# Eight projection slabs with a Gelu moved from the second attention into the stage of the recurrence

## The chip, the cores and the metric

The kernel runs on one core of one Trainium2 chip. A core has five engines, each working through its own queue in order: TensorE (PE) for matmuls, VectorE (DVE), ScalarE (ACT) for functions from tables, GpSimd (POOL) and SyncE (SP), which here issues the DMAs. They wait for one another by semaphores. The metric is the device time of one execution in microseconds, median of several.

## The reference

Two transformer-like blocks of width 1024 over 512 positions, in float32. The change lies in the first half of the second block:

```python
u, g_lru, q, k, v, z = jnp.split(rmsnorm(x) @ w_in, ...)   # 1024, 1024, 1024, 256, 256, 2048 wide
uc  = centred_depthwise_conv(u, conv_w, conv_b)
h   = rg_lru(uc, ..., reverse=False) + rg_lru(uc, ..., reverse=True)
y_a = h * gelu(g_lru)
y_b = banded_alibi_sink_attention(q, k, v, sink)           # 16 heads of 64, blocks of 128, neighbours on both sides
gates = sigmoid(z + b_gate)                                # two of 1024
x = x + (gates[0] * y_a + gates[1] * y_b) @ w_out
```

`rg_lru` is a gated linear recurrence over the positions: r and i are sigmoids of block-diagonal products of uc, a = exp(-8 r softplus(-lam)), b = sqrt(1 - a^2) i uc, h[t] = a[t] h[t-1] + b[t].

## The kernel before

All activations lie transposed, channels on the 128 partitions, 512 positions along a row, so a width of 1024 is eight tiles (DC = 8). Weights come as a stream of 232 slabs of 512 KB, each eight tiles of 128 x 128, in one fixed order (`ORDER`, L71). Each slab goes through four steps. SP loads it into `raw`, which has two places, once VectorE has done the split of the slab two before (L384 to 386). ScalarE rounds it into `w_hi` (`split`, L473), VectorE subtracts to get the rest `w_lo` (`split`, L782); these two have four places, and ScalarE's split also waits until the slab four before is multiplied (L479). TensorE multiplies high x high, high x low and low x high, 24 matmuls of 512 columns for eight tiles (`gemm`, L1371, matmuls L1386 to L1388), into one of the two banks of `gp`. It waits for `w_lo_ready` of the slab and for the output that last had the bank to be read (`FREED`, L278 to L290). Each engine calls its split of slab n + 2 (AHEAD = 2) where it comes to slab n in its own written order, so the order of calls in each engine's code is the order of the work. There is no planner.

The second attention works in 16 units (4 blocks of positions x 2 pairs of key heads x 2 halves). Unit u: scores of unit u + 2 on TensorE (L1509), logits and their maximum on VectorE (L1048 to L1059), exponentials on ScalarE (L563 to L567), transposes of the probabilities (L1537) copied by ScalarE (L588), the inverse of the sums spread over the partitions (L1520), the product with the values (L1548), the outputs copied by ScalarE (L572) and scaled by VectorE (L1070). Blocks 0 and 3 have two key blocks, 1 and 2 three. Between the units stands `between(u)`: one projection slab each. Even units take a tile of u: evacuation with the scale R (L1100) and convolution (L1260 to L1266). Odd units take a tile of g_lru: evacuation into G2 (L1254), ScalarE's Gelu on it (L684), and the split of the convolved tile into `h_hi` (L682) and `h_lo` (called at L1255, the operation is L821). TensorE's `between(u + 1)` stands ahead of the spread inverse and the value product of unit u (L1542). ScalarE runs `exponentials(u + 2)` and then `gate(u + 1)` (L593 to L596); VectorE runs `inverse_sums(u + 1)`, `outputs(u - 1)`, `logits(u + 2)` and then `between(u + 1)` (L1082 to L1092).

The stage of the recurrence goes over eight tiles t. The slabs come in the order `MIX` (L60): at even t one slab of recurrence gates for two tiles (`lru`), then `zb` of tile t, then `za` of tile t - 1. ScalarE (L700 to L732): wait until VectorE has freed the recurrence's buffers (`lru_free`), four sigmoids L710, two tanh L714, two exponentials L717, a square root L720 behind VectorE's clamp, then the splits and the gates' sigmoids (`mix_gate`, L693). VectorE (L1294 to L1323): clamp L1296, two products L1298, L1302, L1305, two scans L1307 and L1308, their sum L1309 (this increments `lru_free`), then the splits, the evacuations `gate_product` (L1279), the product with G2 (L1315), and `gated_attention` and `merged`. The recurrence's buffers `lru` exist once. Then `out2` multiplies the merged tiles by w_out, from `h_hi` and `h_lo`.

Of the kernel before, what the change touches and what calls it, by code (L numbers as in the profile page):

```python
# [20 lines left out]
ALU = mybir.AluOpType  # L21
# [32 lines left out]

_counts = [("u", 4), ("k", 1), ("v", 1), ("gate_a", 8), ("q", 4), ("gate_s", 8), ("branch_a", 4),
           ("glu", 2), ("branch_s", 4), ("out", 8), ("ff", 16 * FF1_PARTS),
           ("q2", 8), ("k2", 2), ("v2", 2), ("u2", 8), ("g2", 8), ("mix", 20),
           ("out2", 8), ("ff2", sum(2 * c + 8 for c in FF2_CHUNKS))]

MIX = []  # L60
for _t in range(DC):
    MIX += ([("lru", _t // 2)] if _t % 2 == 0 else []) + [("zb", _t)] + ([("za", _t - 1)] if _t else [])
MIX += [("za", DC - 1)]
SLAB, _n = {}, 0
for _name, _c in _counts:
    SLAB[_name] = _n
# [2 lines left out]
COUNT = dict(_counts)  # L69

ORDER = list(range(NSLAB))  # L71
for _k in range(8):
    ORDER[SLAB["u2"] + 2 * _k], ORDER[SLAB["u2"] + 2 * _k + 1] = SLAB["u2"] + _k, SLAB["g2"] + _k
assert NSLAB % RING == 0


_outs = [("u", 4), ("k", 1), ("v", 1), ("gate_a", 8), ("q", 4), ("gate_s", 8), ("branch_a", 8), ("glu", 4),
         ("branch_s", 8), ("out", 8), ("ff", 16 * FF1_PARTS), ("q2", 8), ("k2", 2), ("v2", 2), ("u2", 8),
         ("g2", 8), ("mix", 16), ("out2", 8), ("ff2", sum(2 * c + 8 for c in FF2_CHUNKS))]
OUT, _n = {}, 0  # L80
for _name, _c in _outs:
    OUT[_name] = _n
    _n += _c

MIX_SLAB = {key: SLAB["mix"] + i for i, key in enumerate(MIX)}
MIX_OUT = {key: OUT["mix"] + i for i, key in enumerate(k for k in MIX if k[0] != "lru")}

MIX_GATE = [g for t in range(1, DC + 1) for g in [("zb", t - 1)] + ([("za", t - 2)] if t > 1 else [])] + [("za", DC - 1)]


_cols = [("g_mix_pre", 8), ("g_mix_post", 8), ("g_mlp_pre", 8), ("g_mlp_post", 8), ("sinks", 8), ("d_skip", 4),
# [18 lines left out]
def build(nc, slabs, params, s5p, s5bt, s5b, s5c, bias1, nd2, x_in, out):  # L110

    ctx = ExitStack()
    with ctx:
# [152 lines left out]
        H_AT = {"z": 0, "y1": 4, "z2": 12, "ff": 16, "uc": 48, "m2": 56, "ff2": 64}  # L266
        V_AT = {"ff": 0, "uc": 32, "m2": 40, "ff2": 48}
        X_AT = {"post1": 0, "post2": 8, "ff2": 16}
        G_AT = {"gate_a": 0, "gate_s": 8, "g2": 16, "mix": 24, "ff2": 40}
        MIX_VAL = {key: G_AT["mix"] + i + 1 for i, key in enumerate(MIX_GATE)}  # L270
        PART1 = 2 * FF1_PART + DC - FF1_PART
        PART2 = 2 * FF2_CHUNKS[0] + DC
# [6 lines left out]
        for _name, _c in _outs:  # L279
            for _k in range(_c):  # L280
                _o = OUT[_name] + _k
                if _name in ("ff", "q2") and 2 <= _k < START_BANKS:
                    PLACE[_o] = mp, _k - 2
                elif _name in ("gate_s", "u2", "g2"):
# [17 lines left out]
        class Attention:  # L302
# [21 lines left out]
            def lanes(self, u):  # L324


                hp = self.units[u][2]
                return [(i, i % 2, 2 * hp + i // 2, 2 * (i % 2) + i // 2) for i in range(4)]

            def scores(self, i):  # L330
                return mp[:, i, :] if i < 3 else gp[:, 1, :]
# [138 lines left out]
        def _(act):  # L470
# [81 lines left out]
            def attention(A, slab0, gate):  # L552

                for pp in range(A.pairs):
                    act.wait_ge(vt_done, pp + 1 + (A.u0 > 0))
                    nc.scalar.activation(A.vt[:, pp, :, :].rearrange("p a b -> p (a b)"), mp[:, 3 + pp, :],
                                         ACT.Copy).then_inc(vt_ready, 1)

                def exponentials(u):
                    row = mini[u % 3]  # L560
                    lo, hi = A.span(u)
                    act.wait_ge(nb_ready, A.u0 + u + 1)
                    nc.scalar.activation(row[:, 3, :], row[:, 2, :], ACT.Exp)  # L563
                    for h in range(4):
                        L = A.logit[u % 2][:, h, lo:hi]
                        ins = nc.scalar.activation(L, L, ACT.Exp, bias=row[:, 1, h:h + 1], scale=0.125,  # L566
                                                   accum_out=row[:, 4, h:h + 1])  # L567
                    ins.then_inc(ex_done, 1)

                def take_outputs(u):  # L570
                    act.wait_ge(at_done, A.u0 + u + 1)
                    nc.scalar.activation(A.of_heads(A.q, u), by_heads(mp[:, 5, 0:2 * P]), ACT.Copy).then_inc(at_copied, 1)  # L572

                def outputs_hi(u):
                    act.wait_ge(at_read, A.u0 + u + 1)
                    nc.scalar.activation(A.of_heads(h_hi, u), A.of_heads(A.q, u), ACT.Copy).then_inc(h_hi_ready, 1)

                n = len(A.units)
                split(slab0 + AHEAD)
                exponentials(0)  # L580
                exponentials(1)
                gate(0)
                for u in range(n):
                    if u:
                        take_outputs(u - 1)
                    for g, j, _ in A.chunks[u]:
                        act.wait_ge(pt_done, g + 1)
                        nc.scalar.activation(A.pt[:, j, :], mp[:, 3 + g % 2, :], ACT.Copy).then_inc(pt_ready, 1)  # L588
                    if A.name and u:
                        outputs_hi(u - 1)  # L590
                    if u + 1 < n:
                        split(slab0 + u + 1 + AHEAD)
                    if u + 2 < n:  # L593
                        exponentials(u + 2)
                    if u + 1 < n:
                        gate(u + 1)  # L596
                take_outputs(n - 1)
                if A.name:
                    outputs_hi(n - 1)
# [77 lines left out]
            def inputs2(u):  # L677

                m = u // 2
                if u % 2:  # L680
                    act.wait_ge(h_val, V_AT["uc"] + m + 1)
                    nc.scalar.activation(h_hi[:, m, :], UC[:, m, :], ACT.Copy).then_inc(h_hi_ready, 1)  # L682
                    act.wait_ge(out_read, OUT["u2"] + u + 1)
                    nc.scalar.activation(G2[:, m, :], G2[:, m, :], ACT.Gelu_apprx_tanh).then_inc(gate_val, 1)  # L684
            attention(att2, SLAB["u2"], inputs2)


            act.wait_ge(decay_ready, 1)

            def mix_gate(kind, t):  # L690
                row, bias = {"za": (1, 0), "zb": (0, 8)}[kind]
                act.wait_ge(out_read, MIX_OUT[kind, t] + 1)
                nc.scalar.activation(tmp[row], tmp[row], ACT.Sigmoid, bias=col("b_gate", bias + t)).then_inc(gate_val, 1)  # L693
# [6 lines left out]
            for t in range(DC):  # L700
# [18 lines left out]
                act.wait_ge(lru_mid, t + 1)  # L719
                nc.scalar.activation(lru45, lru45, ACT.Sqrt).then_inc(lru_root, 1)  # L720

                split(MIX_SLAB["zb", t] + AHEAD)
                if t >= 1:
                    mix_gate("zb", t - 1)
# [53 lines left out]
        def _(dve):  # L778
# [471 lines left out]
            def inputs2(u):  # L1250

                m = u // 2
                if u % 2:
                    evacuate("u2", u, G2[:, m, :])  # L1254
                    h_low(H_AT["uc"] + m, m, UC[:, m, :])  # L1255
                    return
                x, y = tmp[m % 2], UC[:, m, :]
                evacuate("u2", u, x)
                dve.wait_ge(out_read, OUT["u2"] + u + 1)
# [8 lines left out]
            dve.wait_ge(decay_ready, 1)  # L1268
            dve.wait_ge(s_nd, 16)
            attention(att2, inputs2)  # L1270
            dve.wait_ge(gate_val, G_AT["g2"] + DC)
            dve.wait_ge(at_read, att2.u0 + len(att2.units))


            def gate_product(kind, t, row):

                split(MIX_SLAB[kind, t] + AHEAD)
                dve.wait_ge(half_done, 2 * (MIX_SLAB[kind, t] + 1))
                TT(row, gp[:, MIX_OUT[kind, t] % 2, :], R[:, :], ALU.mult).then_inc(out_read, 1)  # L1279

            def gated_attention(t):
                dve.wait_ge(gate_val, MIX_VAL["zb", t])
# [1 line left out]

            def merged(t):
                dve.wait_ge(gate_val, MIX_VAL["za", t])
                V.run(TT(HS[:, t, :], HS[:, t, :], tmp[1], ALU.mult))
                TT(Q2[:, t, :], Q2[:, t, :], HS[:, t, :], ALU.add).then_inc(h_val, 1)

# [2 lines left out]

            split(MIX_SLAB["lru", 0] + AHEAD)
            for t in range(DC):  # L1294
                dve.wait_ge(lru_tanh, t + 1)
                TS(lru45, lru45, 0.0, None, ALU.max).then_inc(lru_mid, 1)  # L1296
                for d in range(2):
# [10 lines left out]
                V.run(dve.tensor_tensor_scan(lru[5][:, ::-1], lru[2][:, ::-1], lru[3][:, ::-1], 0.0, ALU.mult, ALU.add))  # L1308
                TT(HS[:, t, :], HS[:, t, :], lru[5], ALU.add).then_inc(lru_free, 1)  # L1309

                if t >= 1:
                    gated_attention(t - 1)
                gate_product("zb", t, tmp[0])
                dve.wait_ge(lru_free, t + 1)
                V.run(TT(HS[:, t, :], HS[:, t, :], G2[:, t, :], ALU.mult))  # L1315
                if t >= 2:
                    merged(t - 2)
                if t >= 1:
# [51 lines left out]
        def _(pe):  # L1370
# [232 lines left out]
                    a_stage(name, k)  # L1603
            pe.wait_ge(out_read, OUT["v2"] + 2)
            transpose_values(att2)
            attention(att2, lambda u: a_stage("u2", u))

            def recurrence_gates(j):

# [15 lines left out]
                    else:  # L1625
                        ins.then_inc(half_done, 2)

            for kind, t in MIX:
                if kind == "lru":
                    recurrence_gates(t)  # L1630
                else:
                    gemm("mix", MIX_SLAB[kind, t] - SLAB["mix"], 8, 1, a, al, first=MIX_OUT[kind, t] - OUT["mix"])
# [166 lines left out]
```

## Time and profile before

| | us |
|---|---|
| median of 3 runs (lowest, highest) | 1565.99 (1565.07, 1566.47) |
| profiled execution, its own time | 1568.46 |
| its span, first to last instruction | 1566.7 |
| PE busy | 1440.7 (92%) |
| DVE busy | 944.7 (60%) |
| ACT busy | 603.2 (39%) |
| POOL busy | 84.8 (5%) |
| mean granted TensorE clock | 0.962 of full |

Busy time is the time in which an engine ran instructions; waits, branches and DMA issues are not in it. A busy share is a mean over the kernel's stages, and says nothing of what a single stage waits for. In a timeline, the bracket behind a row gives the idle time of that engine ahead of it and what ended it.

### The profile page before, as it was taken

The page shows a single profiled execution, that of the slowest core. Times are in us where ns is not written, and L with a number is a line of the kernel's source. Part 1 is how long each engine was busy: PE and PEld are TensorE (multiplying, and loading weights), DVE is VectorE, ACT ScalarE, POOL GpSimd, SP SyncE. Part 2 cuts the span into 40 slices and gives each one's busy share as a digit, 9 for nine tenths or more (in the row PEclk, how much of TensorE's full clock was granted, in tenths as well). Part 3 has the DMA queues.
Part 4 walks back from the last instruction along what each step waited for, and adds up shares of the span by engine and source line. Part 5 has one row for each costly group of instructions (what it writes and reads, how often), then busy time and mean ns, then how long its engine had stood idle before and what let it go on. Part 6 is the DMA issues. An engine that isn't in the chain of part 4 may idle for free.

```text
span 1566.7 us, 17487 instructions
## 1 busy us (share of the span) xinstructions
PE 1440.7 (92%) x7088; PEld 1157.3 (74%) x7088; DVE 944.7 (60%) x1339; ACT 603.2 (39%) x932; POOL 84.8 (5%) x69
## 2 busy tenths in 40 slices
PE   4668999999999999999899999968899999999997
PEld 3556777777778888888687777756678888888886
DVE  6999856464564536354746887568875443443445
ACT  4112245333331313123424767778843231222232
POOL 3744100000000000000000000000000000000000
PEclk8889999999999999999899999989999999999998
DMA  4112231223133333333131111122233333333323
GB/s 165 63 55 60 92 105 55 81 82 107 46 108 87 102 94 94 108 90 99 54 101 61 54 54 52 45 67 81 67 96 93 95 107 94 95 94 108 93 84 106
DMA packets 36624, 132.92 MB, mean 85 GB/s; under 512 B 4112, under 2 KB 4240, under 8 KB 36288
## 3 DMA queue, kind: packets, MB, share of 16 engines
q1 hardware_dynamic: 35712, 126.89, 27.2%
q0 software_dynamic: 832, 4.92, 0.9%
q8 instruction: 56, 0.92, 0.2%
q14 instruction: 24, 0.20, 0.0%
HBM read 129.70 MB, written 2.10 MB: 84 GB/s over the span
## 4 chain that ended last, share of the span: by engine, by line
PE 68%; DVE 19%; ACT 8%; issue 3%; DMA 1%; SPq 0%; DVEq 0%; ACTq 0%
PE gp L1386 20%; PE gp L1388 20%; PE gp L1387 20%; DVE w_lo L787 2%; PE mp L1537 2%; PE mp L1509 1%; PE mp L1548 1%; ACT arena L710 1%; PE mp L1520 1%; PE mp L1415 1%; ACT a_hi L507 1%; ACT w_hi L480 1%; DVE arena L1027 1%; ACT arena L714 1%; DVE arena L1305 1%
## 5 line engine op out<-in xcount | busy, mean ns | idle before, releaser
L1386 PE MATMUL gp<-a_hi,w_hi 128*128 128x512 f32 x1120 | 448.2, 400 | 44.2 <-DVE arena L1027 27.3
L1387 PE MATMUL gp<-a_lo,w_hi 128*128 128x512 f32 x1120 | 442.6, 395 | 0.0
L1388 PE MATMUL gp<-a_hi,w_lo 128*128 128x512 f32 x1120 | 442.4, 395 | 0.0
L787 DVE TENSOR_TENSOR w_lo<-raw,w_hi 128x1024 fp32r<-128x1024 f32 x232 | 286.8, 1237 | 124.5 <-ACT w_hi L480 123.2
L480 ACT ACTIVATE w_hi<-raw 128x1024 fp32r<-128x1024 f32 x232 | 242.5, 1050 | 229.5 <-DMA raw<-slabs 162.8
L1386 PEld LDWEIGHTS gp<-a_hi,w_hi 128*128 128x128 f32 x1120 | 214.6, 192 | 98.7 <-DVE w_lo L787 36.5
L1388 PEld LDWEIGHTS gp<-a_hi,w_lo 128*128 128x128 f32 x1120 | 214.1, 191 | 46.0
L1387 PEld LDWEIGHTS gp<-a_lo,w_hi 128*128 128x128 f32 x1120 | 214.9, 192 | 43.9
L1386 PE MATMUL gp<-h_hi,w_hi 128*128 128x512 f32 x576 | 224.9, 390 | 8.9 <-DVE h_lo L821 3.4
L1387 PE MATMUL gp<-h_lo,w_hi 128*128 128x512 f32 x576 | 224.1, 389 | 0.0
L1388 PE MATMUL gp<-h_hi,w_lo 128*128 128x512 f32 x576 | 224.1, 389 | 0.0
L1386 PEld LDWEIGHTS gp<-h_hi,w_hi 128*128 128x128 f32 x576 | 108.1, 188 | 34.1 <-DVE h_lo L821 5.0
L1388 PEld LDWEIGHTS gp<-h_hi,w_lo 128*128 128x128 f32 x576 | 108.1, 188 | 22.6
L1387 PEld LDWEIGHTS gp<-h_lo,w_hi 128*128 128x128 f32 x576 | 108.1, 188 | 22.3
L1348 DVE TENSOR_TENSOR arena<-gp,R 128x512 f32<-128x512 f32 x44 | 30.4, 692 | 69.0 <-PE gp L1388 68.9
L650 ACT ACTIVATE h_hi<-arena 128x512 fp32r<-128x512 f32 x32 | 20.2, 633 | 133.7 <-DVE arena L1181 133.7
L821 DVE TENSOR_TENSOR h_lo<-arena,h_hi 128x512 fp32r<-128x512 f32 x78 | 53.4, 685 | 11.5 <-ACT h_hi L682 6.4
L1206 DVE TENSOR_TENSOR arena<-arena,gp 128x512 f32<-128x512 f32 x24 | 16.5, 687 | 65.8 <-PE gp L1388 65.8
L1442 PE MATMUL gp<-a_hi,w_hi 128*128 128x512 f32 x48 | 23.4, 488 | 32.4 <-DVE a_lo L816 20.7
L763 ACT ACTIVATE h_hi<-arena 128x512 fp32r<-128x512 f32 x22 | 13.9, 633 | 99.5 <-DVE arena L1351 99.5
L1357 DVE TENSOR_TENSOR arena<-arena,gp 128x512 f32<-128x512 f32 x24 | 16.5, 686 | 57.9 <-PE gp L1388 57.9
L566 ACT ACTIVATE arena<-arena 128x256 f32<-128x256 f32 (+2 forms) x96 | 49.8, 520 | 0.0
(266 smaller groups left out, 1525.2 us busy)
## 6 DMA issues: line engine op xcount, KB each, us to landing
raw<-slabs SPq DMA_DIRECT2D x232, 512.0 KB, 3.6
arena<-x_in SPq DMA_DIRECT2D x4, 512.0 KB, 7.3
arena<-x_in POOLq DMA_DIRECT2D x1, 2048.0 KB, 8.3
out_t<-arena SPq DMA_DIRECT2D x8, 256.0 KB, 2.2
arena<-bias POOLq DMA_DIRECT2D x1, 1024.0 KB, 5.3
arena<-s5p SPq DMA_DIRECT2D x3, 264.0 KB, 7.8
arena<-s5b POOLq DMA_DIRECT2D x2, 256.0 KB, 3.3
arena<-s5c POOLq DMA_DIRECT2D x2, 256.0 KB, 4.1
```

The costliest lines, as they stand in the source:

```text
L480: nc.scalar.activation(w_hi[:, n % RING, :], raw[:, n % RAW, :], ACT.Copy).then_inc(w_hi_ready, 1)
L566: ins = nc.scalar.activation(L, L, ACT.Exp, bias=row[:, 1, h:h + 1], scale=0.125, accum_out=row[:, 4, h:h + 1])
L650: nc.scalar.activation(h_hi[:, k, :], fbuf[k % 2], ACT.Copy).then_inc(h_hi_ready, 1)
L787: TT(w_lo[:, n % RING, :], raw[:, n % RAW, :], w_hi[:, n % RING, :].bitcast(F32), ALU.subtract).then_inc(w_lo_ready, 1)
L821: TT(at(h_lo, chunk), src, at(h_hi, chunk).bitcast(F32), ALU.subtract).then_inc(h_lo_ready, 1)
L1206: TT(Fo[:, m, :], Fo[:, m, :], src, ALU.add).then_inc(out_read, 1)
L1348: TT(tmp[e], take("ff2", s0 + 2 * c + e), R[:, :], ALU.mult).then_inc(out_read, 1)
L1386: pe.matmul(dst, hi, x_hi(t), start=t == 0, stop=False)
L1387: pe.matmul(dst, hi, x_lo(t), start=False, stop=False)
L1388: ins = pe.matmul(dst, lo, x_hi(t), start=False, stop=t == tiles - 1)
L1442: pe.matmul(bank(name, e), hi, a(c), start=c == 0, stop=False)
L1537: ins = pe.transpose(mp[:, 3 + g % 2, h * P:(h + 1) * P], A.logit[u % 2][:, h, j * P:(j + 1) * P], ident)
```

## The change

The eight slabs of g_lru leave the attention and come into the recurrence's stage, one per tile, as `("gl", t)` ahead of `("zb", t)`. In the attention every second unit (the odd ones) has no slab. The evacuation of gl stands on VectorE at the top of the tile, without a split of its own; the split of the slab two behind it stands behind the recurrence's last addition. ScalarE's Gelu follows the square root. The product with G2 moves into `merged`. All outputs of the stage alternate between the two banks of `gp`.

```diff
-           ("q2", 8), ("k2", 2), ("v2", 2), ("u2", 8), ("g2", 8), ("mix", 20),
+           ("q2", 8), ("k2", 2), ("v2", 2), ("u2", 8), ("mix", 28),
+STAGE = [key for kind, t in MIX for key in ([("gl", t)] if kind == "zb" else []) + [(kind, t)]]
-for _k in range(8):
-    ORDER[SLAB["u2"] + 2 * _k], ORDER[SLAB["u2"] + 2 * _k + 1] = SLAB["u2"] + _k, SLAB["g2"] + _k
+FILE_G2, FILE_MIX = SLAB["mix"], SLAB["mix"] + DC
+for _i, (_kind, _t) in enumerate(STAGE):
+    ORDER[SLAB["mix"] + _i] = FILE_G2 + _t if _kind == "gl" else FILE_MIX + MIX.index((_kind, _t))
...
-MIX_GATE = [g for t in range(1, DC + 1) for g in [("zb", t - 1)] + ([("za", t - 2)] if t > 1 else [])] + [("za", DC - 1)]
+MIX_GATE = [g for t in range(DC + 1) for g in ([("gl", t)] if t < DC else []) + ([("zb", t - 1)] if t else []) + ([("za", t - 2)] if t > 1 else [])] + [("za", DC - 1)]
...
+            def has_slab(self, u):
+                return self.name != "" or u % 2 == 0
+            def slab(self, u):
+                return u if self.name else u // 2
...
-                    if u + 1 < n:
-                        split(slab0 + u + 1 + AHEAD)
+                    if u + 1 < n and A.has_slab(u + 1):
+                        split(slab0 + A.slab(u + 1) + AHEAD)
...
-                    act.wait_ge(out_read, OUT["u2"] + u + 1)
-                    nc.scalar.activation(G2[:, m, :], G2[:, m, :], ACT.Gelu_apprx_tanh).then_inc(gate_val, 1)
...
+                if kind == "gl":
+                    act.wait_ge(out_read, MIX_OUT[kind, t] + 1)
+                    nc.scalar.activation(G2[:, t, :], G2[:, t, :], ACT.Gelu_apprx_tanh).then_inc(gate_val, 1)
+                    return
...
+                split(MIX_SLAB["gl", t] + AHEAD)
+                mix_gate("gl", t)
                 split(MIX_SLAB["zb", t] + AHEAD)
...
-                    evacuate("u2", u, G2[:, m, :])
                     h_low(H_AT["uc"] + m, m, UC[:, m, :])
...
-            dve.wait_ge(gate_val, G_AT["g2"] + DC)
...
-            def gate_product(kind, t, row):
-                split(MIX_SLAB[kind, t] + AHEAD)
+            def gate_product(kind, t, row, with_split=True):
+                if with_split:
+                    split(MIX_SLAB[kind, t] + AHEAD)
...
+                V.run(TT(HS[:, t, :], HS[:, t, :], G2[:, t, :], ALU.mult))
                 V.run(TT(HS[:, t, :], HS[:, t, :], tmp[1], ALU.mult))
...
             for t in range(DC):
+                gate_product("gl", t, G2[:, t, :], False)
                 dve.wait_ge(lru_tanh, t + 1)
                 TS(lru45, lru45, 0.0, None, ALU.max).then_inc(lru_mid, 1)
...
                 TT(HS[:, t, :], HS[:, t, :], lru[5], ALU.add).then_inc(lru_free, 1)
+                split(MIX_SLAB["gl", t] + AHEAD)
                 if t >= 1:
                     gated_attention(t - 1)
                 gate_product("zb", t, tmp[0])
                 dve.wait_ge(lru_free, t + 1)
-                V.run(TT(HS[:, t, :], HS[:, t, :], G2[:, t, :], ALU.mult))
...
-            attention(att2, lambda u: a_stage("u2", u))
+            attention(att2, lambda u: a_stage("u2", u // 2) if u % 2 == 0 else None)
-            for kind, t in MIX:
+            for kind, t in STAGE:
```

## Rows read from the trace of the kernel before

**Rows 1.** The page, part 4: the chain that ended last, by engine
```profile
PE 68%; DVE 19%; ACT 8%; issue 3%; DMA 1%; SPq 0%; DVEq 0%; ACTq 0%
```

**Rows 2.** Busy time by stretch: length, PE, PEld, DVE, ACT, POOL, clock, DMA
```profile
838.00:1000.00 162.00, 158.55 (x953) 116.86 (x953) 125.20 (x253) 109.69 (x249) 0.00 (x0) 0.99 0.18 53
1000.00:1152.20 152.20, 124.99 (x502) 99.13 (x502) 118.51 (x156) 115.72 (x142) 0.00 (x0) 0.92 0.24 70
```

**Rows 3.** Timeline of TensorE, attention: start, length, line [idle before <-releaser]
```profile
942.28 0.48 PE L1386 MATMUL gp<-a_hi,w_hi 128*128 128x512 f32 x1
...
947.95 0.66 PE L1520 MATMUL mp<-par,arena 128*64 128x128 f32 x8
```

**Rows 4.** Timeline of VectorE, attention
```profile
848.94 0.55 DVE L1260 TENSOR_SCALAR arena<-arena,par 128x512 f32<-128x512 f32 x1
...
939.15 0.69 DVE L821 TENSOR_TENSOR h_lo<-arena,h_hi 128x512 fp32r<-128x512 f32 x1 [1.35 <-ACT h_hi L682]
...
942.56 1.48 DVE L1048 SCALAR_TENSOR_TENSOR arena<-arena,mp 128x384 f32<-128x384 f32 x3 [0.78 <-PE mp L1537]
...
946.81 1.22 DVE L787 TENSOR_TENSOR w_lo<-raw,w_hi 128x1024 fp32r<-128x1024 f32 x1
...
948.78 0.55 DVE L1260 TENSOR_SCALAR arena<-arena,par 128x512 f32<-128x512 f32 x1
...
951.61 0.15 DVE L1064 TENSOR_TENSOR arena<-arena 128x4 f32<-128x4 f32 x1
...
952.61 1.08 DVE L1048 SCALAR_TENSOR_TENSOR arena<-arena,mp 128x256 f32<-128x256 f32 x3 [0.33 <-PE mp L1537]
...
987.71 0.55 DVE L1260 TENSOR_SCALAR arena<-arena,par 128x512 f32<-128x512 f32 x1
```

**Rows 5.** Timeline of ScalarE, attention
```profile
936.00 0.21 ACT L563 ACTIVATE arena<-arena 128x4 f32<-128x4 f32 x1 [2.82 <-DVE arena L1059]
...
955.91 0.20 ACT L563 ACTIVATE arena<-arena 128x4 f32<-128x4 f32 x1 [1.75 <-DVE arena L1059]
...
958.00 0.61 ACT L682 ACTIVATE h_hi<-arena 128x512 fp32r<-128x512 f32 x1
```

**Rows 6.** Groups by line, attention (836 to 1000 us): busy us, mean ns
```profile
L684 ACT ACT_TABLE_LOAD x8 | 10.3, 1283 | 0.1
```

**Rows 7.** Timeline of TensorE, stage of the recurrence
```profile
999.93 0.47 PE L1620 MATMUL mp<-h_hi,w_hi 128*128 128x512 f32 x1 [1.02 <-DVE arena L1070]
...
1054.37 0.77 PE L1386 MATMUL gp<-a_hi,w_hi 128*128 128x512 f32 x1 [3.62 <-DVE arena L1279]
1054.93 0.63 PE L1387 MATMUL gp<-a_lo,w_hi 128*128 128x512 f32 x1
...
1059.20 0.63 PE L1388 MATMUL gp<-a_hi,w_lo 128*128 128x512 f32 x1
...
1152.17 0.50 PE L1386 MATMUL gp<-h_hi,w_hi 128*128 128x512 f32 x1 [1.52 <-DVE h_lo L821]
```

**Rows 8.** Timeline of VectorE, stage of the recurrence
```profile
1015.47 0.69 DVE L1309 TENSOR_TENSOR arena<-arena 128x512 f32<-128x512 f32 x1
...
1051.07 0.69 DVE L1309 TENSOR_TENSOR arena<-arena 128x512 f32<-128x512 f32 x1
...
1065.67 0.69 DVE L1309 TENSOR_TENSOR arena<-arena 128x512 f32<-128x512 f32 x1
...
1081.69 1.29 DVE L1302 SCALAR_TENSOR_TENSOR arena<-arena 128x512 f32<-128x512 f32 x2 [3.13 <-ACT arena L720]
...
1086.72 0.69 DVE L1309 TENSOR_TENSOR arena<-arena 128x512 f32<-128x512 f32 x1
...
1136.87 0.69 DVE L1309 TENSOR_TENSOR arena<-arena 128x512 f32<-128x512 f32 x1
```

**Rows 9.** Timeline of ScalarE, stage of the recurrence
```profile
1071.89 1.06 ACT L480 ACTIVATE w_hi<-raw 128x1024 fp32r<-128x1024 f32 x1 [6.22 <-DMA raw<-slabs]
```

**Rows 10.** Busy time by stretch, columns as in rows 2
```profile
1056.00:1060.00 4.00, 4.00 (x11) 3.09 (x11) 3.81 (x6) 3.96 (x5) 0.00 (x0) 0.53 0.52 154
```

More of the change, by code:

```diff
@@ L78 @@
          ("branch_s", 8), ("out", 8), ("ff", 16 * FF1_PARTS), ("q2", 8), ("k2", 2), ("v2", 2), ("u2", 8),
-         ("g2", 8), ("mix", 16), ("out2", 8), ("ff2", sum(2 * c + 8 for c in FF2_CHUNKS))]
+         ("mix", 24), ("out2", 8), ("ff2", sum(2 * c + 8 for c in FF2_CHUNKS))]
 OUT, _n = {}, 0
@@ L83 @@
     _n += _c
-MIX_SLAB = {key: SLAB["mix"] + i for i, key in enumerate(MIX)}
-MIX_OUT = {key: OUT["mix"] + i for i, key in enumerate(k for k in MIX if k[0] != "lru")}
-MIX_GATE = [g for t in range(1, DC + 1) for g in [("zb", t - 1)] + ([("za", t - 2)] if t > 1 else [])] + [("za", DC - 1)]
+MIX_SLAB = {key: SLAB["mix"] + i for i, key in enumerate(STAGE)}
+MIX_OUT = {key: OUT["mix"] + i for i, key in enumerate(k for k in STAGE if k[0] != "lru")}
+MIX_GATE = [g for t in range(DC + 1) for g in ([("gl", t)] if t < DC else []) + ([("zb", t - 1)] if t else []) + ([("za", t - 2)] if t > 1 else [])] + [("za", DC - 1)]
 _cols = [("g_mix_pre", 8), ("g_mix_post", 8), ("g_mlp_pre", 8), ("g_mlp_post", 8), ("sinks", 8), ("d_skip", 4),
@@ L268, in build @@
         X_AT = {"post1": 0, "post2": 8, "ff2": 16}
-        G_AT = {"gate_a": 0, "gate_s": 8, "g2": 16, "mix": 24, "ff2": 40}
+        G_AT = {"gate_a": 0, "gate_s": 8, "mix": 16, "ff2": 40}
         MIX_VAL = {key: G_AT["mix"] + i + 1 for i, key in enumerate(MIX_GATE)}
@@ L283, in build @@
                     PLACE[_o] = mp, _k - 2
-                elif _name in ("gate_s", "u2", "g2"):
+                elif _name in ("gate_s", "u2"):
                     PLACE[_o] = gp, 0
@@ L1257, in inputs2 @@
                 x, y = tmp[m % 2], UC[:, m, :]
-                evacuate("u2", u, x)
-                dve.wait_ge(out_read, OUT["u2"] + u + 1)
+                evacuate("u2", m, x)
+                dve.wait_ge(out_read, OUT["u2"] + m + 1)
                 V.run(TS(y, x, col("conv_w", 16 + m), col("conv_b", m), ALU.mult, ALU.add))
@@ L1270, in _ @@
             attention(att2, inputs2)
-            dve.wait_ge(gate_val, G_AT["g2"] + DC)
             dve.wait_ge(at_read, att2.u0 + len(att2.units))
-            def gate_product(kind, t, row):
-                split(MIX_SLAB[kind, t] + AHEAD)
+            def gate_product(kind, t, row, with_split=True):
+                if with_split:
+                    split(MIX_SLAB[kind, t] + AHEAD)
                 dve.wait_ge(half_done, 2 * (MIX_SLAB[kind, t] + 1))
-                TT(row, gp[:, MIX_OUT[kind, t] % 2, :], R[:, :], ALU.mult).then_inc(out_read, 1)
+                TT(row, bank("mix", MIX_OUT[kind, t] - OUT["mix"]), R[:, :], ALU.mult).then_inc(out_read, 1)
             def gated_attention(t):
```

## The prediction, made before the changed kernel was run

> **What bounds the kernel now.** I read the chain that ended last first: TensorE holds 68% of it, VectorE 19%, ScalarE 8% [rows 1]. The change touches two stages, so the next view is the busy time in each. In the second attention (838 to 1000 us) TensorE is busy 158.6 of 162 us: it is the bound. In the stage of the recurrence (1000 to 1152.2 us) it is busy 125.0 of 152.2, and none of the four is full [rows 2]. The idea on paper is to carry eight slabs from the full stage to the one with 27 us of idle TensorE. What it is worth hangs on what the two loops wait for once they are rearranged, so I followed both in the timelines, instruction by instruction.
>
> **Part 1, the attention without eight slabs.** A slab of 24 matmuls takes 5.67 us from its first matmul to the work behind it [rows 3]. Eight of them are 45 us, and that would be the gain if TensorE stayed the bound. It doesn't. Between the convolution of one even unit and that of the next, VectorE has one serial chain, because it works in order and waits inside it for ScalarE. For units with three key blocks, by its pieces [rows 4, 5]:
> - inverse sums and outputs: 0.67 us (951.61 to 952.61, less the 0.33 it waited)
> - logits, maximum and small operations: 942.56 to 946.81, 4.25
> - ScalarE's exponentials and the copy of L682, for which `h_low` waits (the copy stands behind the exponentials in its queue): 936.00 to 939.15, 3.15
> - `h_low` 0.6; inverse sums and outputs again 0.67; the next logits 4.25
> - split and evacuation of the slab that stays, 946.81 to 948.78, 1.97; convolution to 951.61, 2.83.
>
> The sum is 18.4. The loop that runs through TensorE (logits 4.3, exponentials and copy 3.2, ScalarE's output and probability copies 0.9, the third transpose 0.5, slab 5.7, evacuation, convolution, inverse and outputs 4.2) gives 18.8; I take 18.7. With two key blocks the logits to the maximum take 3.30 (952.61 to 955.91) and the exponentials 2.09 (to 958.00): 16.0. VectorE's wait for L682 was 1.35 us (the row at 939.15); the split and evacuation that go (1.9 us) only hid the rest of that wait, so removing them lengthens it. The true gain here is the Gelu with its table load between the copy and the outputs (L684, 8 loads, 10.3 us of ScalarE in the stage [rows 6]) and TensorE's shorter rounds. The seven intervals between eight convolutions last 848.94 to 987.71, 138.8 us; new they are 3 x 16.0 + 4 x 18.7 = 122.8, so 16 less. At the end unit 14 has no slab: the last outputs follow the convolution after outputs, 1.6 us of matmuls, a transpose round and ScalarE's copy, near 996.1 and not 999.93 (the first recurrence matmul [rows 7]): 3.8 less. Sum **-19.8 us**. Bounds: 0 if new waits eat it; -40 if TensorE's own work stays the bound (eight slabs less the last few us). I take -19.8, as it is made of this trace's own rows.
>
> **Part 2, the recurrence with three slabs a tile.** Call F the end of L1309 of a tile (the addition behind the scans, which frees the recurrence's buffers). Now F of tile 0 is 1016.2, that of tile 7 1137.6; tiles alternate between 14.6 us (odd) and 21 (even) [rows 8]. TensorE's need per pair of tiles rises from 5 slabs to 7, 38.2 us at 5.45, against 35.6 that a pair lasts now. That alone adds about 3 us a pair. The order adds more:
> - `gate_product("gl", t)` stands at the top of the tile on VectorE, ahead of the clamp L1296. The clamp, the square root (ScalarE), both products, the scans and so F are queued behind the wait for slab gl.
> - The order of the slabs is (lru), gl, zb, za, and each is split two ahead. The split of the slab za is now the first thing behind F on VectorE. TensorE has by then done zb and waits for it; then it must do za, in even tiles lru, and gl, in that order, before the clamp may go.
>
> So F to F, even tile: split and start 1.3; three slabs 16.4; evacuation 0.7 and clamp 0.65; square root and the products 1.3; L1302 to the end of L1309, 1081.69 to 1087.41, 5.7. Sum 26.1 (21 now). Odd tile: 1.3, two slabs 10.9, 0.7, 0.65; ScalarE is then the later one: its raw slab lands 3.7 us behind the split at F + 1.2, it splits, copies, runs the four sigmoids (2.4), two tanh, table load, two exponentials, table load, and is free at F + 14.2; square root 1.1, then 5.7: 21.1 (14.6 now). The new Gelu, its table load and the moved ScalarE split (1.28 + 0.63 + 1.05) stand between the square root and F + 0.8, ahead of the wait for that raw slab, which ends at F + 4.9: they cost nothing. If that cover went, it would be 3 us a tile. The product with G2 (0.68) moves within VectorE's queue behind F, where TensorE is the later one: nothing. The DMAs keep their number and order rule; SP issues each on the split two slabs before, and the 6.22 us that ScalarE waits for one in even tiles now [rows 9] is covered by the longer TensorE stretch. POOL has nothing here.
>
> Stage at full clock: tile 0, lru and gl 10.9 from 999.93, then 0.7, 0.65, 1.3 and 5.7: F at 1019.3, 3.1 later. Tile 1: 15.1 (no za yet). Three pairs of 47.2. F of tile 7 is 1019.3 + 15.1 + 141.6 = 1176.0, +38.4. Behind it one more slab is waited for before the last gate (za 6, za 7, last product): the next stage's last input (now at 1152.17, 14.6 behind F) comes at about 17.9, +3.3.
>
> **The clock.** TensorE idles each tile from the end of zb to F + 1.3, about 4.2 us. The trace shows what that does: after idles of 3.6 to 3.9 us (1054.37 and two like it) the granted clock is about half of full (0.53 in 1056 to 1060 us [rows 10]), the lower of its two levels, 1.2 GHz, and matmuls start every 0.43 us, not 0.23: 12 of them here (1054.93 to 1059.20 [rows 7]), 9 and 13 in the same view at the two others. That is 1.8 to 2.6 us, mean 2.2. After idles of 0.3 to 1.5 us nothing of the kind is seen. Today this lies beside the recurrence chain; new it lies on it: 2.2 in tile 1 and in each even tile, 1.7 in an odd one (ScalarE's slack takes the rest), 2.2 + 3 x 3.9 = 13.9, and 0.9 in the tail. So part 2 is 38.4 + 13.9 + 3.3 + 0.9 = **+56.5 us**. The Trainium skill, "TensorE: Matmul & The Clock Gate", section "HAM oscillation", speaks against the change in the same way: short waits repeated in every round make each round begin at the low clock. The same page ("Wait — 56ns, not 53.3ns?") has warm matmuls of 512 columns start every 215.7 ns; by that a slab is 5.2 us and the sum would be some 5 us smaller, but the rows here show 227 and I go by them.
>
> **Sum.** -19.8 + 56.5 = +36.7. The profiled execution took 1568.46 us with a span of 1566.7; the median of the three runs is 1565.99. On that median it gives 1602.7; I say **1602**.
>
> **Rivals.**
> - *TensorE is the bound of the recurrence stage* and takes the slabs into its gaps (faster). It needs za split before F, or VectorE's top wait to be over when ScalarE's tanh is. Then the stage grows by 43.6 less its 27.2 of idle, and the low-clock phases go (41 matmuls, counted in that view, x 0.2 = 8.2): +8.2 - 19.8 = -11.6, 1554. For it: VectorE and ScalarE would be busy about 35 us of a 38 us pair, so neither forbids it. Against: the order written out above. It decides once TensorE's idle per tile is under 1 us. Chance 0.07.
> - *The clock holds*, the rest as forecast: 1566.0 - 19.8 + 41.7 = 1588. For it: the idles are set by my small terms; against: all three idles of this length were followed by the lower level. 0.18.
> - *The attention gives more*, near TensorE's own work (-35): 1587. Against: the wait of `h_low` stands in the code and the trace. 0.10.
> - *The attention gives nothing*, since idles of 2 to 3 us lower the clock there too or the third transpose waits longer: 1618 to 1622. 0.06.
> - *The units don't lose what they should* (the change doesn't do what it says): the counts and the order leave even units with a slab and odd ones with none, and eight slabs are still multiplied, so I give it 0.01, at 1566.
>
> My forecast has 0.58. The range: from 1584 (the clock holds or the attention gives more, some us below either) to 1614. A measurement of this kernel can tell about 0.2% from no change. Faster only by the first rival, 0.07; within 0.2%, 0.02; slower, 0.91.
>
> **What would show it.** In the profile after: convolutions (L1260) 16 and 18.7 us apart; F to F of 23 (odd) and 28 (even), TensorE idle 4 us ahead of each za, released by VectorE's split; VectorE idle for the evacuation of gl, released by TensorE, some 1 us in odd and 5 or more in even tiles; matmuls of 0.43 us after each idle. Wrong, if F to F is near 19 for all tiles (TensorE full), if L1260 is 14 apart, or if ScalarE is what the clamp and the root wait for in even tiles.

## The result, and the profile after

The changed kernel takes 1611.73 us (median of 4 runs, 1611.03 to 1613.39) against 1565.53 before: a ratio of 1.0296, 95% interval 1.0279 to 1.0314, slower by 46.2 us. The forecast was slower, 1602, range 1584 to 1614. The profiled execution took 1611.34 us with a span of 1609.5, 42.8 more than the span before; the profiled execution of before lay 2.9 us above the median of its runs and that of the changed kernel 0.4 below, which is the rest of the difference to a few tenths.

Busy time by stretch of the changed kernel, columns as in [rows 2], first the attention, then the stage of the recurrence:

```profile
838.00:989.40 151.40, 123.80 (x768) 88.32 (x769) 111.00 (x243) 78.40 (x220) 0.00 (x0) 0.93 0.10 29
989.40:1196.50 207.10, 174.87 (x693) 140.34 (x693) 133.48 (x172) 140.05 (x166) 0.00 (x0) 0.92 0.25 72
```

The attention is only 10.6 us shorter (162.0 to 151.4), though 34.8 us of TensorE's busy time left it, and its clock fell from 0.99 to 0.93. The recurrence's stage grew by 54.9 us (152.2 to 207.1), though only 43.6 us of slabs came in; TensorE is idle for 32 us of it, more than before. So TensorE sets the pace of neither stage. The timelines name what does.

TensorE in the attention, timeline of the changed kernel (L1553 transposes, L1536 spreads the inverses, L599 is ScalarE's copy of probabilities, L1085 VectorE's scaling of outputs, L1636 the first recurrence matmul):

```profile
867.63 1.12 PE L1536 MATMUL mp<-par,arena 128*64 128x128 f32 x8 [4.12 <-DVE arena L1085]
...
893.91 0.66 PE L1553 MATMUL mp<-par,arena 128*128 128x128 f32 x4 [3.58 <-ACT arena L599]
...
914.93 0.84 PE L1553 MATMUL mp<-par,arena 128*128 128x128 f32 x4 [3.92 <-ACT arena L599]
...
954.99 0.66 PE L1553 MATMUL mp<-par,arena 128*128 128x128 f32 x4 [2.86 <-ACT arena L599]
...
982.83 0.66 PE L1536 MATMUL mp<-par,arena 128*64 128x128 f32 x8 [3.92 <-DVE arena L1085]
...
989.43 0.47 PE L1636 MATMUL mp<-h_hi,w_hi 128*128 128x512 f32 x1 [1.03 <-DVE arena L1085]
```

Five times (1.05 to 3.92 us) TensorE stands at the third transpose for a copy that waits behind the exponentials in ScalarE's queue. VectorE waits there too. After the four longer of these waits (2.86 to 3.92 us) 24 of the slabs' matmuls take 0.63 us, the time of the low clock, where 0.39 is that of the full one. VectorE's view of the same place, convolutions (L1274) and `h_low` (L836), the rows that answer to [rows 4]:

```profile
848.61 0.55 DVE L1274 TENSOR_SCALAR arena<-arena,par 128x512 f32<-128x512 f32 x1
...
882.22 0.55 DVE L1274 TENSOR_SCALAR arena<-arena,par 128x512 f32<-128x512 f32 x1
...
893.14 0.69 DVE L836 TENSOR_TENSOR h_lo<-arena,h_hi 128x512 fp32r<-128x512 f32 x1 [3.18 <-ACT h_hi L693]
...
902.39 0.55 DVE L1274 TENSOR_SCALAR arena<-arena,par 128x512 f32<-128x512 f32 x1
...
979.19 0.55 DVE L1274 TENSOR_SCALAR arena<-arena,par 128x512 f32<-128x512 f32 x1
```

The wait of `h_low` grew from 1.35 to 3.18 us, and 882.22 to 902.39 is 20.2 us for a pair with three key blocks. The seven intervals between the eight convolutions take 15.4, 18.2, 20.2, 21.0, 20.9, 19.1 and 15.7 us, 130.6 in all, 138.8 before.

The recurrence, VectorE: the evacuation of gl at the top of the tile (L1293 ahead of L1312, the clamp) and L1325, whose end is F, in an even and an odd tile:

```profile
1024.84 0.69 DVE L1325 TENSOR_TENSOR arena<-arena 128x512 f32<-128x512 f32 x1
...
1045.05 0.69 DVE L1293 TENSOR_TENSOR arena<-gp,R 128x512 f32<-128x512 f32 x1 [9.05 <-PE gp L1404]
1045.65 0.68 DVE L1312 TENSOR_SCALAR arena<-arena 128x1024 f32<-128x1024 f32 x1
...
1052.50 0.69 DVE L1325 TENSOR_TENSOR arena<-arena 128x512 f32<-128x512 f32 x1
...
1067.23 0.69 DVE L1293 TENSOR_TENSOR arena<-gp,R 128x512 f32<-128x512 f32 x1 [4.75 <-PE gp L1404]
...
1074.68 0.69 DVE L1325 TENSOR_TENSOR arena<-arena 128x512 f32<-128x512 f32 x1
...
1103.44 0.69 DVE L1325 TENSOR_TENSOR arena<-arena 128x512 f32<-128x512 f32 x1
...
1176.66 0.69 DVE L1325 TENSOR_TENSOR arena<-arena 128x512 f32<-128x512 f32 x1
```

VectorE waits 9.05 and 4.75 us for slab gl in these two tiles, 8.45 in the later even ones and 4.15 in the later odd ones; F to F is 27.7 to 28.9 us in even tiles and 22.2 in odd ones. TensorE, in front of slab za and in the matmuls behind it, and the last input of the next stage:

```profile
1076.56 0.80 PE L1402 MATMUL gp<-a_hi,w_hi 128*128 128x512 f32 x1 [3.94 <-DVE w_lo L802]
1077.16 0.63 PE L1403 MATMUL gp<-a_lo,w_hi 128*128 128x512 f32 x1
...
1196.52 0.50 PE L1402 MATMUL gp<-h_hi,w_hi 128*128 128x512 f32 x1 [0.67 <-DVE h_lo L836]
```

Eight such idles of 3.93 to 4.00 us, all ended by the split L802 right behind F, are 31.6 us, and 65 matmuls behind them take 0.63 us (0.39 at full clock), and start 0.43 us apart and not 0.23.

### The profile page after: what moved, and what is told of

Same layout as the page of the kernel before. It is cut to its first block, busy times and chain, and to the rows that moved or that the text cites. A ratio compares the mean times of both kernels' runs of the same rounds, so it can differ in the third digit from the quotient of the medians.

```text
span 1609.5 us, 17480 instructions
## 1 busy us (share of the span) xinstructions
PE 1453.3 (90%) x7088; PEld 1167.9 (73%) x7088; DVE 944.7 (59%) x1339; ACT 595.1 (37%) x925; POOL 84.8 (5%) x69
## 4 chain that ended last, share of the span: by engine, by line
PE 69%; DVE 23%; ACT 4%; issue 3%; DMA 1%; SPq 0%; DVEq 0%; ACTq 0%
PE gp L1402 21%; PE gp L1403 20%; PE gp L1404 20%; DVE w_lo L802 3%; DVE arena L1063 1%; DVE arena L1070 1%; PE mp L1553 1%; ACT arena L577 1%; PE mp L1564 1%; ACT a_hi L518 1%; PE mp L1431 1%; DVE arena L1042 1%; PE mp L1525 1%; DVE arena L1321 1%; ACT w_hi L491 1%
## 5 line engine op out<-in xcount | busy, mean ns | idle before, releaser
L1403 PE MATMUL gp<-a_lo,w_hi 128*128 128x512 f32 x1120 | 447.2, 399 | 0.0
L802 DVE TENSOR_TENSOR w_lo<-raw,w_hi 128x1024 fp32r<-128x1024 f32 x232 | 287.0, 1238 | 126.9 <-ACT w_hi L491 125.3
L1364 DVE TENSOR_TENSOR arena<-gp,R 128x512 f32<-128x512 f32 x44 | 30.4, 692 | 68.9 <-PE gp L1404 68.9
L661 ACT ACTIVATE h_hi<-arena 128x512 fp32r<-128x512 f32 x32 | 20.2, 633 | 133.7 <-DVE arena L1196 133.7
L836 DVE TENSOR_TENSOR h_lo<-arena,h_hi 128x512 fp32r<-128x512 f32 x78 | 53.5, 687 | 26.2 <-ACT h_hi L693 21.0
L1293 DVE TENSOR_TENSOR arena<-gp,R 128x512 f32<-128x512 f32 x24 | 16.5, 689 | 66.7 <-PE gp L1404 66.7
L778 ACT ACTIVATE h_hi<-arena 128x512 fp32r<-128x512 f32 x22 | 13.9, 633 | 99.5 <-DVE arena L1367 99.5
```

What stands on the lines that cost most here:

```text
L661: nc.scalar.activation(h_hi[:, k, :], fbuf[k % 2], ACT.Copy).then_inc(h_hi_ready, 1)
L802: TT(w_lo[:, n % RING, :], raw[:, n % RAW, :], w_hi[:, n % RING, :].bitcast(F32), ALU.subtract).then_inc(w_lo_ready, 1)
L836: TT(at(h_lo, chunk), src, at(h_hi, chunk).bitcast(F32), ALU.subtract).then_inc(h_lo_ready, 1)
L1293: TT(row, bank("mix", MIX_OUT[kind, t] - OUT["mix"]), R[:, :], ALU.mult).then_inc(out_read, 1)
L1364: TT(tmp[e], take("ff2", s0 + 2 * c + e), R[:, :], ALU.mult).then_inc(out_read, 1)
L1403: pe.matmul(dst, hi, x_lo(t), start=False, stop=False)
```

## The experiments

The runs were made in four groups, and the kernel before was run in each: its median was 1565.5 to 1566.7 us. So a difference of about 1 us between two experiments says nothing.

**The attention half alone.** All of "gl" is left out: its slabs, its evacuation, the Gelu and the product with G2. The second stage has its order of before.

```diff
-STAGE = [key for kind, t in MIX for key in ([("gl", t)] if kind == "zb" else []) + [(kind, t)]]
+STAGE = list(MIX)
...
-                split(MIX_SLAB["gl", t] + AHEAD)
-                mix_gate("gl", t)
...
-                V.run(TT(HS[:, t, :], HS[:, t, :], G2[:, t, :], ALU.mult))
...
-                gate_product("gl", t, G2[:, t, :], False)
...
-                split(MIX_SLAB["gl", t] + AHEAD)
...
-    put(tiles_of(g, None, HEADS2))
```

> Only the attention half of the change: the eight slabs, their evacuation, the Gelu and the product with G2 are left out altogether, and the stage of the recurrence has the order of the kernel before. In the trace of the changed kernel the recurrence starts 10.5 us earlier than before (989.4 against 999.9 us). Theory 1 (that is all the attention gives, because its freed units wait for ScalarE and TensorE then runs at the lower clock): 1555 us, give or take 2. Rival (the attention gives the 20 us of the forecast and something later takes half back): 1546.

Measured: 1555.9 us, ratio 0.9936 (0.9924 to 0.9949), 10.2 us below the kernel before in the same runs (1566.12). Theory 1. The whole gain of freeing eight units is 10 us. The change as a whole costs 46, so the price of the second stage is some 56 us.

**TensorE's idles in the recurrence filled.**

```diff
+            def fill(free, dst, n):
+                pe.wait_ge(out_read, free)
+                for _ in range(n):
+                    pe.matmul(dst, a_hi[:, 0, 0:P], a(0), start=True, stop=True, skip_group_check=True)
...
                     gemm("mix", ...)
+                    if kind == "zb":
+                        nxt = MIX_OUT[kind, t] + 1 - OUT["mix"]
+                        fill(freed_by("mix", nxt), bank("mix", nxt), 14)
```

> The changed kernel with 14 more matmuls of 512 columns on TensorE in every tile of the recurrence, after slab zb, where it idles 3.9 us; their output is overwritten. Theory 1 (the idles bring the lower clock, and the matmuls behind them are on the path): the 65 matmuls of 0.43 us in this stage go, 65 x 0.2 = 13 us, so 1599 to 1600, with F to F near 26 (even) and 21 (odd). Rival (the lower clock has another cause, or the path doesn't run through TensorE there): 1612, or some us more for the added matmuls.

Measured: 1597.07 us, 14.7 below the changed kernel, with 112 matmuls more. Theory 1, and 2 us better than it said. Timelines of TensorE, VectorE and ScalarE around an odd tile:

```profile
1052.59 0.50 PE L1402 MATMUL gp<-a_hi,w_hi 128*128 128x512 f32 x1 [0.76 <-DVE w_lo L802]
...
1073.16 0.50 PE L1402 MATMUL gp<-a_hi,w_hi 128*128 128x512 f32 x1 [0.76 <-DVE w_lo L802]
```

```profile
1050.71 0.69 DVE L1325 TENSOR_TENSOR arena<-arena 128x512 f32<-128x512 f32 x1
...
1063.83 0.69 DVE L1293 TENSOR_TENSOR arena<-gp,R 128x512 f32<-128x512 f32 x1 [4.75 <-PE gp L1404]
...
1071.28 0.69 DVE L1325 TENSOR_TENSOR arena<-arena 128x512 f32<-128x512 f32 x1
```

```profile
1065.15 1.06 ACT L733 ACTIVATE arena<-arena 128x1024 f32<-128x1024 f32 x1 [0.43 <-DVE arena L1312]
```

The idle in front of za is 0.76 us here and under 1 us in all tiles; no matmul of the stage takes 0.63 us any more. F to F is 20.6 to 20.7 (odd) and 26.0 (even), near the forecast's values at full clock, 21.1 and 26.1. The low clock cost what the forecast gave it (13.9, and 0.9 in the tail). In the odd tile the square root waits 0.43 us for the clamp, which waits for slab gl: TensorE, not ScalarE, is the later one there.

**The idles of the attention filled.**

```diff
+                        if x == 2 and not A.name and u % 2:
+                            fill(freed_by("u2", (u + 1) // 2), bank("u2", (u + 1) // 2), 12)
...
+                    if not A.name and u == 2:
+                        fill(freed_by("u2", 2), bank("u2", 2), 12)
+                    if not A.name and u == 14:
+                        fill(freed_by("mix", 0), bank("mix", 0), 12)
                     spread_inverse(u)
```

> The changed kernel with 12 more matmuls in the idles of the second attention: ahead of the third transpose of odd units with three key blocks, and ahead of the spread inverse of units 2 and 14. Theory 1 (low clock takes back part of the attention's gain): 24 matmuls of 0.43 us and some transposes go, 5 to 7 us, so 1605 to 1607, and 18.7 us between two convolutions where it is 20 to 21 now. Rival (the interval is set by the chain VectorE to ScalarE to VectorE alone): 1611 to 1612 and intervals as they are.

Measured: 1606.34 us, 5.4 below the changed kernel. The seven intervals now take 125.9 us (130.6), the longest ones 19.4 to 20.3 where they were 20.2 to 21.0: the theory's time, but its intervals are not down to 18.7, so the clock is a part of what is missing and not all.

**The split of za ahead of the chain.**

```diff
                 ins.then_inc(lru_tanh, 1)
+                split(MIX_SLAB["gl", t] + AHEAD)
...
-                split(MIX_SLAB["gl", t] + AHEAD)
                 mix_gate("gl", t)
...
+                split(MIX_SLAB["gl", t] + AHEAD)
                 gate_product("gl", t, G2[:, t, :], False)
...
                 TT(HS[:, t, :], HS[:, t, :], lru[5], ALU.add).then_inc(lru_free, 1)
-                split(MIX_SLAB["gl", t] + AHEAD)
```

> The changed kernel with the split of the slab two behind gl made ahead of the chain of the recurrence: on ScalarE behind the tanh, on VectorE at the top of the tile, ahead of the evacuation of gl. TensorE can then do za right behind zb, beside the chain. Theory 1 (what costs is that za is done after F and ahead of gl): F to F of 22 (even) and 18 (odd) where it is 28.8 and 22.2 now, low clock gone, 1574 to 1578. Rival A (the wait for gl at the top costs wherever za lies): 1605 or more. Rival B (ScalarE is the limit once TensorE is not, and its split in the chain costs): 1585 to 1592.

Measured: 1575.97 us, 35.8 below the changed kernel, ratio to before 1.0062 (1.0050 to 1.0075). Busy time by stretch, attention and recurrence, and F of tiles 2 and 3:

```profile
838.00:988.40 150.40, 124.33 (x760) 89.00 (x760) 108.92 (x232) 76.25 (x217) 0.00 (x0) 0.92 0.10 29
988.40:1160.20 171.80, 162.79 (x694) 131.14 (x694) 132.91 (x172) 138.78 (x166) 0.00 (x0) 0.98 0.29 86
```

```profile
1046.59 0.69 DVE L1326 TENSOR_TENSOR arena<-arena 128x512 f32<-128x512 f32 x1
...
1063.90 0.69 DVE L1326 TENSOR_TENSOR arena<-arena 128x512 f32<-128x512 f32 x1
```

Theory 1: the time is the forecast one. The stage is 171.8 us, 35.3 less. TensorE has two idles over 2 us in place of eight, and 11 matmuls of 0.63 us in place of 65, so these 35.3 us hold most of what the low clock cost too. F to F is 17.3 us in odd tiles and 22.4 in even ones (23.9 in tile 2), 39.6 to 39.9 for the later pairs against TensorE's 38.2. The wait for gl is still at the top of the tile: it was the late split of za that cost. Even so the stage is 19.6 us longer than before: eight slabs, 43.6 us, don't fit into 27 us of idle.

**The evacuation of gl behind the chain**, alone and with the early split.

```diff
-                mix_gate("gl", t)
...
                     mix_gate("za", t - 2)
+                mix_gate("gl", t)
...
-                gate_product("gl", t, G2[:, t, :], False)
                 dve.wait_ge(lru_tanh, t + 1)
...
                 split(MIX_SLAB["gl", t] + AHEAD)
+                gate_product("gl", t, G2[:, t, :], False)
```

> The changed kernel with VectorE's evacuation of gl moved from the top of the tile to behind the recurrence's last addition, and its Gelu behind the two sigmoids; the splits stay where the change has them, so TensorE still does za after F. Theory (order of za and the wait at the top both lie on the path, the wait adding a slab): F to F of 22 to 24 (even) and 21 (odd) for 28.8 and 22.2, 1585 to 1592. Rival (the wait costs nothing of its own, only the late za does): 1605 or more. Second rival (the wait is all of it): 1575 or less.

> Both together: the split of za ahead of the chain, and the evacuation of gl behind it. With the split alone a pair of tiles takes 39.7 us, and TensorE's own work is 38.2. Theory (the stage is at TensorE's bound, and little is left to gain): 1570 to 1575. Rival (the chain of the recurrence still sets the pace in even tiles): 1565 or less. A third way: ScalarE has one more table load a tile and loses 1 us in each, 1580 or more.

Measured: 1605.17 and 1594.68 us. Both miss. Alone it gave 6.6 us for 20 to 27 expected; with the early split it lost 18.7 us of what that had gained. My theory had overlooked a second duty of that evacuation. TensorE in the run with both, in front of slab za:

```profile
1050.94 0.47 PE L1402 MATMUL gp<-a_hi,w_hi 128*128 128x512 f32 x1 [2.01 <-DVE arena L1293]
```

The releaser is L1293, the evacuation, not L802, the split. The outputs alternate between two banks, so za needs the bank that gl leaves. With the evacuation behind F, za can't start ahead of F, whatever is split. In the run with the late evacuation alone these idles are 1.5 to 7.1 us, all with this releaser. So the wait at the top of the tile is not a mere cost. The first time is that of the first rival, the second that of the third way. ScalarE's rows of the run with both, and VectorE's wait for the square root, show that the third way has a share too:

```profile
1050.83 0.63 ACT L702 ACTIVATE arena<-arena 128x512 f32<-128x512 f32 x1 [1.48 <-DVE arena L1293]
...
1052.43 1.28 ACT L723 ACT_TABLE_LOAD   x1
...
1062.43 1.06 ACT L734 ACTIVATE arena<-arena 128x1024 f32<-128x1024 f32 x1
...
1078.09 1.28 ACT L723 ACT_TABLE_LOAD   x1 [1.79 <-PE mp L1638]
```

```profile
1063.53 1.29 DVE L1318 SCALAR_TENSOR_TENSOR arena<-arena 128x512 f32<-128x512 f32 x2 [1.99 <-ACT arena L734]
```

The Gelu (L702) waits for the evacuation behind F, and from it to the square root (L734) ScalarE works without a pause in this odd tile; VectorE then waits 1.99 us for the root. So F is late because of ScalarE, and za because of F. The order needs five table loads a tile where the changed kernel has four; the one ahead of the sigmoids (L723) takes 1.28 us and in even tiles stands behind a wait for slab lru. How much of the 18.7 us is the bank's and how much ScalarE's wasn't separated. But what TensorE waits for in front of za is the bank, which none of the expectations named.

**The kernel before, filled.** 12 matmuls behind slabs za 1, 3 and 5, into a bank of `mp` that its sigmoid has read.

```diff
+                    if kind == "za" and t % 2 == 1 and t < DC - 1:
+                        pe.wait_ge(lru_sig, 4 * t + 7)
+                        fill(mp[:, (4 * t + 6) % 6, :], 12)
```

> The kernel before, with 12 more matmuls on TensorE in its idle of 3.6 to 3.9 us in three tile pairs of the recurrence, whose output is overwritten. The low clock behind these idles goes. Theory (before the change that clock lies beside the recurrence chain and costs nothing): no change, 1564 to 1568. Rival (it costs there too, 34 matmuls x 0.2 us): 1559 to 1561.

Measured: 1566.43 us against 1566.74, ratio 1.0002 (0.9992 to 1.0011). The time is as the theory said, but the theory's condition, that the low clock goes, wasn't met in full: the three filled idles shrank to 0.8 to 1.0 us and the full clock held there, while low-clock matmuls came up at other places of the stage, in front of the lru slabs among them. Their number in the stage fell from 35 to 25. F to F stayed at 14.6 and 21.0. What it shows is that this work of TensorE has slack in the kernel before; that the low clock costs exactly nothing there is not shown.

**Another order in the attention**, with the early split.

```diff
                     for x, (g, j, _) in enumerate(A.chunks[u]):
...
+                        if x == 1 and not A.name and u % 2 and u + 1 < n:
+                            exponentials(u + 1)
...
-                    if u + 2 < n:
+                    if u + 2 < n and (A.name or u % 2):
                         exponentials(u + 2)
...
+                    swap = not A.name and u % 2
-                    if u + 1 < n:
+                    if u + 1 < n and not swap:
                         inverse_sums(u + 1)
...
+                    if u + 1 < n and swap:
+                        inverse_sums(u + 1)
```

> The split of za ahead of the chain, and in the second attention another order: ScalarE runs the exponentials of even units behind the first two probability copies of the odd unit, not ahead of them, and VectorE takes the logits ahead of the inverse sums in odd units. Theory (the attention's freed units wait for ScalarE's exponentials, first with the copies and h_low, then with the low clock): intervals between convolutions of 16 to 17.5 us for 20 to 21, 14 to 15 for 15 to 19, so 16 to 20 us off the 1576 of the split alone: 1556 to 1560, below the kernel before. Rival (the order of these is not what it waits for): 1574 to 1577.

Measured: 1545.11 us, ratio to before 0.9865 (0.9851 to 0.9880): 31 us below the early split, where 16 to 20 were expected, and 1.4% faster than the kernel before.

```profile
838.00:959.00 121.00, 114.76 (x760) 82.52 (x760) 108.46 (x234) 78.17 (x217) 0.00 (x0) 0.99 0.12 36
959.00:1130.90 171.90, 162.61 (x694) 131.11 (x694) 132.94 (x172) 138.78 (x166) 0.00 (x0) 0.98 0.29 86
```

```profile
959.04 0.47 PE L1641 MATMUL mp<-h_hi,w_hi 128*128 128x512 f32 x1 [1.02 <-DVE arena L1087]
```

```profile
891.01 0.55 DVE L1279 TENSOR_SCALAR arena<-arena,par 128x512 f32<-128x512 f32 x1
...
906.67 0.55 DVE L1279 TENSOR_SCALAR arena<-arena,par 128x512 f32<-128x512 f32 x1
```

The attention takes 121.0 us, 41 less than before, TensorE is busy 95% of it (98% before, 82% in the changed kernel) and the clock is back at 0.99. Intervals with three key blocks are 14.9 to 15.7 us, where I expected 16 to 17.5.

Three more runs take that apart.

> The changed kernel with the new order of the attention alone (ScalarE's exponentials of even units behind two probability copies of the odd unit, VectorE's logits ahead of the inverse sums in odd units); the stage of the recurrence as the change has it. Theory (the two stages' losses are independent and add): 1611.7 less the 30 us by which the order moved the start of the recurrence in the run with both, 1580 to 1583. Rival (part of those 30 us needs the early split): 1590 or more.

Measured: 1582.88 us (1578.26 to 1582.97), ratio 1.0100. This is the theory's time. The new order is worth 29 us on the changed kernel and 31 on the early split: the two stages' losses add.

> Early split, and of the attention's new order only ScalarE's half: exponentials deferred, VectorE's inverse sums stay ahead of outputs and logits. VectorE then still waits for the exponentials once a pair. Theory (both waits count, TensorE's third transpose more): intervals of 17 us with three key blocks, 1553 to 1562, between 1545 and 1576. Rival A (ScalarE's half is all of it): 1545 to 1548. Rival B (VectorE's half is all of it): 1572 or more.

Measured: 1556.88 us (1553.86 to 1562.64), intervals of 17.1 us with three key blocks. ScalarE's half of the order gives 19.1 of the 30.9 us, VectorE's half on top of it 11.8. The runs of this kernel scatter more, but the starts of the recurrence say the same: 988.44, 969.57 and 959.04 us, 18.9 and 10.5 apart. So both waits count, as the theory said, and neither rival holds. VectorE's half without ScalarE's wasn't run.

> The kernel before, with the new order of the attention, slabs in all units as before. Theory (there TensorE is the bound of the attention, and the order has nothing to free): 1562 to 1568, or some us more, since the Gelu's wait for slab g2 now stands ahead of the output copies. Rival (the order is a gain of its own, whatever the slabs): 1550 or less.

Measured: 1565.31 us against 1565.85, ratio 0.9995 (0.9986 to 1.0005). With a slab in every unit the order is worth nothing. It is worth 30 us only where units are freed.

## Why the prediction was right

The direction and the mechanism of the second stage held: +36.7 was forecast, +44.4 is what the profile shows to the same point (the next stage's last input, 1152.17 to 1196.52), and +46.2 the medians. The measured 1611.7 lies near the upper end of the range, and nearly all that is missing is in the attention. By its steps:

- *The recurrence, +56.5.* From its first matmul to the next stage's last input it grew from 152.2 to 207.1, +54.9. Tile 0: 19.3 us from the first matmul to F, 19.4 forecast. Tile 1: 16.8 for 17.3. Even tiles 27.7 to 28.9 for 28.3, odd 22.2 for 22.8. The tail from F to the last input 19.2 for 18.8. The cause, za behind F and ahead of gl, is shown by the early split (-35.8, low clock included), and the low clock by the filled idles (-14.7 for 13.9 + 0.9). Two readings in it were off. VectorE's wait for gl in odd tiles, "some 1 us" among the signs, is 4.15 to 5.75. And at full clock ScalarE was to be the later one in odd tiles (21.1); the filled run shows TensorE there, at 20.6, which is what the forecast's own TensorE terms add up to (20.55). That ScalarE's Gelu, table load and moved split cost nothing in this order was part of the sum. ScalarE's row agrees: behind them it waits 3.99 us for the next raw slab (1057.91) and 1.95 for the clamp (1068.55). It wasn't tested by itself.
- *The attention, -19.8: this term was mis-sized*, it measured -10.5 (the recurrence's first matmul at 989.43 for 999.93), and -10.2 in the run without the second half. The intervals took 130.6 us for my 122.8, the end 10.2 for 8.4. The step that failed is "I take 18.7" for three key blocks, which measured 18.2, 20.2, 21.0 and 20.9: it took the slab at 5.7 us, full clock, while the same sum made TensorE wait for ScalarE's copy ahead of that slab. One of the three intervals counted at 16.0 took 19.1 (944.37 to 963.51): its logits have two key blocks, but a third transpose for a unit of the block before still falls into it and waits 2.86 us (954.99). My sum asked only in the recurrence what an idle does to the clock. Filling the idles gave 5.4 us of the 9.6 missing; the other 4 are not settled. In VectorE's row the 0.6 us that h_low's copy takes and a wait of 1.6 us for the slab (901.67) show part of it.
- *The attention gives nothing* (1618 to 1622, chance 0.06) had the mechanism that my sum lacked: idles that lower the clock there too, and a third transpose that waits longer. Both are in the trace (0.38 to 0.41 us before, up to 3.92 after), but they took half of the gain and not all of it.
- *The clock.* The idles were forecast at about 4.2 us and are 3.9 to 4.0, and they brought the lower of the two levels, 1.2 GHz (a granted clock of 0.50 in 1076.5 to 1082.0 us). The rival in which the full clock holds (1588) is refuted. The Trainium skill, "TensorE: Matmul & The Clock Gate", section "HAM oscillation", describes waits in every round after which each round starts at the low clock. The trace agrees in the main: low-clock matmuls follow all eight idles of the recurrence, though only three of its rounds start with one, and they follow at least four of the waits in the attention. The waits that the Trainium skill tells of there are for a DMA; these are for a split and for a copy.
- *"TensorE is the bound"* (1554) failed for the reason given, the order of the queue. The early split shows how near it was: with one split moved on each of two engines the stage needs 171.8 us. But its price, +8.2, was too low, as it counted all the idle as free: the stage still grew by 19.6, and the kernel stayed slower.
- *The attention gives more, near TensorE's own work.* It didn't, but the bound of -40 is real: with the new order the recurrence starts at 959.04, 40.9 us earlier than before.
- What the prediction didn't see: the two banks. It was not needed for the sum, since the change reads gl early, but it made the expectations of the two runs with the late evacuation miss.

## What to carry to other kernels

Work taken out of a stage is worth only what the next wait in line allows: before moving it, write down the in-order chain of every engine for the emptied round as well as for the filled one, and reorder the emptied one (here ScalarE's exponentials behind two copies and VectorE's logits ahead of the inverse sums, 30 us). Idle of TensorE in another stage is no free place unless the moved work can run beside that stage's serial chain: ask which slab is split, and which bank is read, before the chain ends. If an idle of several microseconds appears in each round, price the matmuls behind it at the low clock in every stage, not only in the one that you suspect.

## What the runs showed of the hardware that was not expected

- More matmuls made the kernel faster: 112 added in the recurrence gave -14.7 us, and the granted clock of that stage went from 0.92 to 1.00.
- The length of an idle alone doesn't fix what follows. In the changed kernel, of the eight idles of 3.9 to 4.0 us five were followed by a first matmul of 0.50 us, three by one of 0.80 us, slow at once; at 1054.38, one of the five, the slow ones came 1.2 us later (1055.57). In the kernel before with filled gaps, low-clock matmuls followed an idle of 2.8 us (1066.43), 1.5 us behind it; with the late evacuation none followed the idles of 2.2 us (1101.20).
